# Gathering a group's eight token chunks in one run, from token halves stored chunk by chunk

## What is computed

```python
def swiglu(h, wg, wu, wd):
    return (jax.nn.silu(h @ wg) * (h @ wu)) @ wd

def moe_ffn(h, router_w, router_bias, exp_gate, exp_up, exp_down, sh_gate, sh_up, sh_down):
    ...
    _, top_e = lax.top_k(jnp.where(emask, choice, -jnp.inf), MOE_TOPK)
    ...
    def step(y, blk):
        tok, wt, e = blk
        out = swiglu(hf[tok], exp_gate[e], exp_up[e], exp_down[e])
        return y.at[tok].add(out.astype(F32) * wt[:, None]), None
    ...
    shared = swiglu(hf, sh_gate, sh_up, sh_down)
    return (y.astype(h.dtype) + shared).reshape(B, S, D)
```

## Time and profile before

| | before |
|---|---|
| median of three runs | 2489.0 us |
| the profiled execution | 2497.49 us |
| its span, first to last instruction | 2495.7 us |
| TensorE busy over the span | 2086.2 us (84%) |
| VectorE busy | 1004.9 us (40%) |
| ScalarE busy | 698.3 us (28%) |
| mean share of the DMA engines, 850 to 1300 us | 0.89 |
| granted TensorE clock, mean | 0.900 |

### The profile page before, as it was taken

How to read it: one execution, slowest core, us unless ns; L and a number is a source line. 1 busy time by engine, 2 the same in 40 slices (tenths; PEclk the granted TensorE clock), 3 DMA queues, 4 the chain that set the end, 5 groups by cost and what they waited for, 6 DMA issues and landing times. The chain is left out here.

```text
span 2495.7 us, 33167 instructions
## 1 busy us (share of the span) xinstructions
PE 2086.2 (84%) x13583; PEld 1670.1 (67%) x13583; DVE 1004.9 (40%) x1329; ACT 698.3 (28%) x926; POOL 19.3 (1%) x20
## 2 busy tenths in 40 slices
PE   4759958898798999999997275788899876887997
PEld 3748957876765555655553274688888865877986
DVE  3465355554522111111111645544435445444344
ACT  2321023112221111111110122332444346323543
POOL 0000000000000000000000200000000000000000
PEclk9857669997899999999999586899999898998999
DMA  9400036541379988889888431243355430432551
GB/s 317 143 18 1 8 122 201 156 135 55 110 282 419 392 354 348 342 344 350 351 352 280 178 122 34 68 141 113 135 174 198 135 119 0 144 126 84 179 176 59
DMA packets 227762, 453.39 MB, mean 182 GB/s; under 512 B 15814, under 2 KB 165108, under 8 KB 209948
## 3 DMA queue, kind: packets, MB, share of 16 engines
q1 hardware_dynamic: 199216, 403.14, 44.5%
q10 hardware_dynamic: 26092, 39.75, 4.6%
q0 software_dynamic: 2304, 8.39, 0.9%
HBM read 511.77 MB, written 25.97 MB: 215 GB/s over the span
## 5 line engine op out<-in xcount | busy, mean ns | idle before, releaser
L1640 PE MATMUL psum<-weight_ring,moe_block_tokens_T 128*64 128x256 f32 x1520 | 347.2, 382 | 11.2 <-issue 10.9
L1641 PE MATMUL psum<-weight_ring,moe_block_tokens_T 128*64 128x256 f32 x1520 | 347.5, 382 | 0.0
L1640 PEld LDWEIGHTS psum<-weight_ring,moe_block_tokens_T 128*64 128x64 f32 x1520 | 208.8, 138 | 160.0 <-issue 66.3
L1641 PEld LDWEIGHTS psum<-weight_ring,moe_block_tokens_T 128*64 128x64 f32 x1520 | 208.8, 138 | 0.0
L1660 PE MATMUL psum<-weight_ring,moe_hidden 128*64 128x512 f32 x760 | 183.8, 605 | 0.0
L1699 ACT ACTIVATE moe_gate_up<-psum 128x256 f32<-128x256 f32 x95 | 36.5, 384 | 467.4 <-PE psum L1641 467.4
L1839 DVE TENSOR_TENSOR moe_hidden<-psum,moe_silu 128x128 f32<-128x128 f32 x95 | 27.7, 292 | 315.5 <-ACT moe_silu L1705 315.5
L1845 DVE COPY moe_block_out<-psum 128x512 f32<-128x512 f32 x95 | 65.7, 692 | 214.0 <-PE psum L1660 212.2
L407 PE MATMUL psum<-mlp_operand_high,mlp_weights_high 128*128 128x256 f32 x480 | 136.7, 285 | 0.0
L407 PE MATMUL psum<-mlp_operand_high,mlp_weights_low 128*128 128x256 f32 x480 | 135.7, 283 | 0.0
L407 PE MATMUL psum<-mlp_operand_low,mlp_weights_high 128*128 128x256 f32 x480 | 135.7, 283 | 0.0
(11 more groups left out here) (759 smaller groups left out, 4905.0 us busy)
## 6 DMA issues: line engine op xcount, KB each, us to landing
weight_ring<-in_exp_gate SPq DMA_DIRECT2D x95, 1024.0 KB
weight_ring<-in_exp_up SPq DMA_DIRECT2D x95, 1024.0 KB
weight_ring<-in_exp_down SPq DMA_DIRECT2D x95, 1024.0 KB
weight_ring<-in_mlp_w SPq DMA_DIRECT2D x64, 1024.0 KB
weight_ring<-in_ada_w SPq DMA_DIRECT2D x24, 1024.0 KB
expert_rows<-moe_block_out ACTq DMA_DIRECT2D x190, 128.0 KB, 6.5
weight_ring<-in_w_in SPq DMA_DIRECT2D x23, 1024.0 KB
weight_ring<-in_xa_wkv SPq DMA_DIRECT2D x16, 1024.0 KB
```

The source lines that it names most:

```text
L1640: nc.tensor.matmul(ps[0:CAP, s % 2, 0:FF], x, wg[:, k, :], start=(k == 0), stop=(k == DC - 1))
L1641: mm = nc.tensor.matmul(ps[CAP:P, s % 2, 0:FF], x, wu[:, k, :], start=(k == 0), stop=(k == DC - 1))
```

## The change

Three things are changed. The token halves are stored chunk by chunk: `xh` and `xl` are now `[P, TT, DC, P]`, and a chunk's 128 elements lie next to each other, so that a weight load reads them contiguously. For that the two operations on ScalarE and the two on VectorE that make the halves read the tokens in another order (`by_chunk`: every eighth element, in eight rounds); they write contiguously. And `chunks_in` gives all eight chunks beside the first block of a group, and none beside the other seven. The number of instructions on every engine is the same.

```diff
-            xh, xl = st.sbuf("tokens_high", [P, TT, D], FR), st.sbuf("tokens_low", [P, TT, D], FR)
+            xh, xl = st.sbuf("tokens_high", [P, TT, DC, P], FR), st.sbuf("tokens_low", [P, TT, DC, P], FR)
...
+            def by_chunk(t):
+                return h2[:, t].rearrange("p (q c) -> p c q", c=DC)
+
...
             def chunks_in(i):
 
-                r = i % GRP
-                if i // GRP + 1 >= NGRP:
-                    return ()
-                return (0, 1) if r == 0 else (r + 1,) if r < GRP - 1 else ()
+                return range(DC) if i % GRP == 0 and i // GRP + 1 < NGRP else ()
...
                             for part in (xh, xl):
-                                mm = nc.tensor.matmul(ps[:, 3 + n % 2, :], part[:, t, bass.DynSlice(c, P, DC)], onehot[:, g % 2, t, :],
+                                mm = nc.tensor.matmul(ps[:, 3 + n % 2, :], part[:, t, c, :], onehot[:, g % 2, t, :],
...
                     for t in range(TT):
-                        nc.scalar.activation(xh[:, t], h2[:, t], ACT.Copy).then_inc(xh_made, 1)
+                        nc.scalar.activation(xh[:, t], by_chunk(t), ACT.Copy).then_inc(xh_made, 1)
...
                         dve.wait_ge(xh_made, t + 1)
-                        v.tensor_tensor(xl[:, t], h2[:, t], xh[:, t].bitcast(F32), ALU.subtract).then_inc(xl_made, 1)
+                        v.tensor_tensor(xl[:, t], by_chunk(t), xh[:, t].bitcast(F32), ALU.subtract).then_inc(xl_made, 1)
```

## The result

The changed kernel takes 2501.26 us (median of 12 runs), the kernel before 2489.64 us (12 runs); the ratio is 1.0044, with a 95% interval of 1.0031 to 1.0057. The forecast was 2484 us, and its range ended at 2498.

A forecast was written before the change was run, and what follows sets the result against it. Fetches bound the expert blocks up to `up(17)`, TensorE those from 850 to 1300 us. -9.6 us there and +4.5 at the start gave -5.1, 2492.4 profiled, 2484 from the median of 2489.0; range 2475 to 2498.

The forecast's parts named there:

- The load at 188 ns: Gather's weight loads, line 1624: contiguous token halves load in near 190 ns, as line 2358 does, instead of 329.
- the starts 0.227 us apart: Gather's matmuls, line 1624: distance between starts falls from 0.246 to 0.227 us, a chunk from 0.98 to 0.91.
- The run: Eight chunks gathered beside a group's first block: 7.55 us, bounds 6.8 and 8.3, against 8.62 for a group's gather before.
- The start: First expert blocks, up to `up(17)`, bound by fetches: the run between `up(1)` and `up(2)` delays loads, costing +4.5 us.
- the gap in the fetches: Sign of being right: DMA engines idle between 720 and 725 us, as the next load is issued 4.7 us later.
- The cover for the strided reads: Making the token halves: slower reads, 1.2 us more on VectorE, hide in idle times of 6.89 (ScalarE) and 7.03 us (VectorE).
- the term of -9.6 us for the second stretch: Expert blocks where TensorE sets the time (profiled 850 to 1300 us): nine groups save 1.07 us each.
- the ring starves behind each run: Rival, 10%: no weight slot is freed during a run, DMA engines fall behind 21 us in nine groups: 2505 us.
- the reason given against that rival: Weight ring: at share 0.89 it keeps up; during a run it can fetch three untaken slots, with up to eight there.
- the gain of 1.07 us a group: Gather of one group, 8.62 to 7.55 us: 0.6 from the layout, the rest from entering once instead of seven times.

The follow-up runs named there:

- layout_only: The changed kernel with the old order, chunks spread over seven blocks, so only the new layout against the kernel before: 2477.56 us, ratio 0.9947.
- half_down_after: The changed kernel with half the down weights not fetched: 2467.06 us, one run; the kernel before with the same cut: 2477.30; from `gate_up(17)` on 9.9 us shorter.

## Why the prediction was wrong

**What held.** The load at 188 ns and the starts 0.227 us apart. The run: 7.55 us forecast, 7.52 measured. The start, in its mechanism: the gap in the fetches is at its place, and the first part is 131.34 - 126.94 = 4.4 us longer. The forecast of +4.5 had counted in that group 0's run ends sooner, which the first part leaves out; from the start of that run to `gate_up(17)` it is 139.90 us before and 143.57 after, 3.7 more, its lower bound. In part the size is luck: the run costs 5.6 us here (131.34 against 125.70), and the layout gives back 1.2 (126.94 to 125.70), which the forecast had at nothing in this stretch. The cover for the strided reads: the two operations on ScalarE take 4.01 us instead of 2.00, the two on VectorE 3.94 instead of 2.36, 1.6 us more and not the 1.2 that line 1436 had let expect, but both engines still idle behind them for over 4 us:

```profile
670.39 4.01 ACT L1714 ACTIVATE moe_tokens_high<-moe_tokens 128x1024 fp32r<-128x1024 f32 x2 [0.47 <-PEq L383]
...
679.90 0.60 ACT L1716 ACTIVATE moe_block_out<-psum 128x512 f32<-128x512 f32 x1 [4.20 <-PE psum L1595]
...
678.18 3.94 DVE L1765 TENSOR_TENSOR moe_tokens_low<-moe_tokens,moe_tokens_high 128x1024 fp32r<-128x1024 f32 x2
...
686.88 0.69 DVE L1768 TENSOR_TENSOR moe_block_out<-psum,moe_block_out 128x512 f32<-128x512 f32 x1 [4.77 <-PE psum L1595]
```

**What failed** is the term of -9.6 us for the second stretch. It took a group to be TensorE's work, 8 x 5.69 + 7.55 = 53.1 us, and left the fetches out since the share was 0.89. Measured is +8.2 us. The difference, 17.8 us, is the waits for weights: the nine groups exceed 53.03 us by 18.2 in all. It is what the rival "the ring starves behind each run" says, which had 10% and a price of 21 us (2505; measured 2501). That its price came out so near is luck in part: it took the DMA engines at 0.89 behind the run, as before, where they ran full (1.02 and 416 GB/s from 912 to 929 us); the loss is in the run itself.

**The step that was wrong** is the reason given against that rival: "during the run of 7.55 us it can fetch three slots that nobody takes, and up to eight are there". It counts slots as if they stood full or on order when the run begins. They don't: ahead of the run at 895.6 us the last load that moves bytes is issued 3.5 us before it and is done by 902 us. The sum that should have been made is one line for the DMA engines, as there was one for TensorE. A group fetches 16 slots on average (two blocks of three) and stores eight outputs: 16 x 1.049 + 8 x 0.262 = 18.9 MB, 45.1 us at 418 GB/s. Around this run, from 900 to 912 us, the engines move 107 GB/s x 12 us = 1.28 MB, work for 3.1 us: 8.9 us are lost. 45.1 + 8.9 = 54.0 us, more than TensorE's 53.0, before any rest is counted that is lost elsewhere; this group takes 55.36.

Over all nine groups of the changed kernel the bytes take 45.6 us at 418 GB/s and 7.5 are lost behind the run, together as much as the 53.0 of TensorE's own work; the groups take 55.0, as 1.9 more are lost elsewhere. So the sum says in the mean that the slack is gone, and no more. It doesn't give each group's time: the first has 47.4 us of bytes and loses 4.4 behind its run, and takes 54.94 all the same. Why the groups differ so little is not worked out.

What is lost is not made up either. By the rival's own figures two fetching blocks and three stores take 16.9 us at the full rate, and TensorE asks for them every 17.07: the seven blocks behind a run leave next to nothing over. A mean share of 0.89 left 11% of 54.14 us free, 6 us a group (8.5 us, if what is missing to 418 GB/s is counted). It lay in gaps of some 3 us, one in three blocks; a run makes one long gap of it, and the ring of eight slots can't carry that over.

The trace of before had most of what this needed. SyncE's rows show that one slot is freed about every 2.3 us and that a load that fetches is issued at once: the ring is never more than its slots ahead, a third of them go to further blocks that fetch nothing, and what matters is not how much is on order on average but for how long no slot is freed. That is the run, the transposes and `down`, 0.4 + 7.5 + 1.8 = 9.7 us, and 13.2 us from one `up` to the next.

**A size that was off, without harm to the sum**: of the gain of 1.07 us a group 0.6 was put down to the layout and the rest, nearly half, to entering the gather once instead of seven times. layout_only shows a gain of 1.19 us by the layout alone, and the run adds none. The cost of entering was the exposed strided load, and went with it. So the 9.9 us of half_down_after lie near the forecast's 9.6 by luck: one half was too small and the other isn't there. Had this been seen, the change would have been forecast in two halves, one of them worth nothing to TensorE and with a risk on the fetches.

## What to carry to other kernels

Before work is gathered into a run on the engine that frees a prefetch ring's slots, make the sum for the transfers too: bytes of a period at the full rate, plus the time in which no slot is freed less what is really on order then; where that comes up to the engine's own period, as here, expect the run to be paid for in waits, which in this kernel appear 20 to 44 us behind its end. A mean DMA share of 0.9 is no slack for a burst. And take a change that has two parts apart: here the layout alone gives 0.53%, by a contiguous read of the stationary operand, and the new order spends more than that.

## What the runs showed of the hardware

- A load of 128 fp32r columns takes 329 ns with a stride of 32 bytes and 188 ns contiguously. Under a matmul of 512 columns the difference shows as 0.246 against 0.23 us between starts; where the load is exposed, behind two short transposes, it is 0.12 us (0.44 against 0.32).
- Reading 1024 fp32 elements of SBUF with a stride of 32 bytes costs ScalarE 2.0 us in place of 1.0 and VectorE 2.0 in place of 1.2, in an operation whose output is contiguous. Read once and loaded as weights 192 times for each half, the price is well spent.
- With one slot more in the ring the changed order's second part goes from 8.2 us longer than before to 7.5 us shorter (each against its own partner), while the old order's doesn't move (515.71 and 516.08).
